# Moving a sum of squares from GpSimd to VectorE, and another order for the start of attention, in a two-block model on one core

## The reference, cut to what matters

```python
hx = modulate(rmsnorm(x, g), sh1, sc1)          # 512 x 1024
hc = modulate(rmsnorm(ctx, g), csh1, csc1)      # 256 x 1024
cq  = rmsnorm(hx @ w_dq, g_q)                   # 512 x 512
q   = (cq @ w_uq).reshape(16 heads, 64 + 32)    # the last 32 turned by position (rope)
kv  = hx @ w_dkv                                # 512 x 288, the same for hc
ckv = rmsnorm(kv[:, :256], g_kv)
k_pe = rope(kv[:, 256:])                        # one 32-wide part, shared by all heads
k   = concat(ckv @ w_uk, k_pe)                  # keys of context + x: 768
v   = ckv @ w_uv                                # 768 x 16 heads x 64
p   = softmax(q @ k.T / sqrt(96))               # per head, 512 x 768
x   = x + g1 * ((p @ v) @ w_o)
```

## Time and profile before

| | |
|---|---|
| median of 3 runs | 1750.52 us (1746.06 to 1751.31) |
| the profiled execution | 1746.06 us, its span 1744.3 us |
| mean granted TensorE clock | 0.993 |
| busy: PE, DVE, ACT, POOL | 98%, 59%, 32%, 58% |
| DMA | 217.19 MB, mean 125 GB/s |

### The profile page before, as it was taken

How to read it: one execution, slowest core, us unless ns; L and a number is a source line. 1 busy time by engine, 2 the same in 40 slices (tenths; PEclk the granted TensorE clock), 3 DMA queues, 4 the chain that set the end, 5 groups by cost and what they waited for, 6 DMA issues and landing times.

```text
span 1744.3 us, 24852 instructions
## 1 busy us (share of the span) xinstructions
PE 1708.5 (98%) x9190; PEld 1417.0 (81%) x9190; DVE 1027.0 (59%) x1514; ACT 560.4 (32%) x1019; POOL 1016.2 (58%) x675
## 2 busy tenths in 40 slices
PE   9999999999999999996999999999999999999998
PEld 7877888798888777786888898888888898787887
DVE  3456777677867743424487547655558259437183
ACT  4557777533233232112223124222212121113111
POOL 3447667556665665562666256666666634447663
PEclk9999999999999999998999999999999999999999
DMA  8223323133278853334223133334433362213332
GB/s 350 76 68 102 115 88 109 37 95 96 87 249 297 276 186 109 109 122 181 87 96 96 31 103 104 120 110 168 144 124 136 103 239 65 61 61 101 97 94 89
DMA packets 56183, 217.19 MB, mean 125 GB/s; under 512 B 6241, under 2 KB 8545, under 8 KB 53026
## 3 DMA queue, kind: packets, MB, share of 16 engines
q1 hardware_dynamic: 51058, 201.80, 34.5%
q10 hardware_dynamic: 5040, 14.22, 2.1%
HBM read 201.84 MB, written 14.16 MB: 124 GB/s over the span
## 4 chain that ended last, share of the span: by engine, by line
PE 91%; DVE 2%; POOL 2%; DMA 2%; ACT 1%; issue 1%; SPq 0%; POOLq 0%; DVEq 0%; ACTq 0%
PE PS L2010 27%; PE PS L2012 26%; PE PS L2011 26%; PE PS L2341 2%; PE PS L2357 2%; PE PS L770 2%; PE PS L1420 1%; POOL WL L1928 1%; DMA RAW<-in_whin 1%; PE PS L1404 1%; PE PS L557 1%; PE PS L1423 1%; PE PS L2164 0%; POOL WH L1925 0%; DMA X<-in_x 0%
## 5 line engine op out<-in xcount | busy, mean ns | idle before, releaser
L1928 POOL TENSOR_TENSOR WL<-RAW,WH 128x1024 fp32r<-128x1024 f32 (+3 forms) x233 | 599.3, 2572 | 19.4
L2010 PE MATMUL PS<-HH,WH 128*128 128x512 f32 (+1 forms) x1400 | 530.8, 379 | 19.4 <-POOL WL L1928 17.4
L2012 PE MATMUL PS<-HH,WL 128*128 128x512 f32 (+1 forms) x1400 | 525.2, 375 | 0.0
L2011 PE MATMUL PS<-HL,WH 128*128 128x512 f32 (+1 forms) x1400 | 525.0, 375 | 0.0
L1925 POOL TENSOR_SCALAR WH<-RAW 128x1024 fp32r<-128x1024 f32 (+3 forms) x233 | 258.4, 1109 | 331.6 <-PE PS L2012 297.0
L2010 PEld LDWEIGHTS PS<-HH,WH 128*128 128x128 f32 x1400 | 263.9, 189 | 76.7 <-POOL WL L1928 20.1
L2012 PEld LDWEIGHTS PS<-HH,WL 128*128 128x128 f32 x1400 | 263.9, 188 | 47.8
L2011 PEld LDWEIGHTS PS<-HL,WH 128*128 128x128 f32 x1400 | 264.1, 189 | 45.6
L1924 POOL TENSOR_TENSOR SC<-ONES 1x1 f32<-1x1 f32 x134 | 30.6, 229 | 286.3 <-PE PS L2012 261.5
L1953 POOL TENSOR_SCALAR PR<-PR,SC 128x768 f32<-128x768 f32 x47 | 109.5, 2337 | 69.8 <-DVE SC L3047 69.8
L2010 PE MATMUL PS<-HIDH,WH 128*128 128x512 f32 (+1 forms) x396 | 148.4, 375 | 0.0
(11 more groups left out here) (435 smaller groups left out, 2801.0 us busy)
## 6 DMA issues: line engine op xcount, KB each, us to landing
RAW<-in_wup SPq DMA_DIRECT2D x88, 512.0 KB, 3.6
MRF<-in_modw SPq DMA_DIRECT2D x52, 512.0 KB, 4.5
RAW<-in_wdn SPq DMA_DIRECT2D x32, 704.0 KB, 4.1
MR<-in_modw SPq DMA_DIRECT2D x28, 512.0 KB, 3.6
RAW<-in_whin SPq DMA_DIRECT2D x28, 512.0 KB, 3.6
MK<-in_modk SPq DMA_DIRECT2D x8, 1024.0 KB, 10.4
RAW<-in_whead SPq DMA_DIRECT2D x8, 640.0 KB, 4.6
RAW<-in_wo SPq DMA_DIRECT2D x8, 512.0 KB, 3.6
```

Source lines behind the costliest of these rows:

```text
L1928: pool.tensor_tensor(WL[s][:, 0:n], raw[:, 0:n], WH[s][:, 0:n].bitcast(F32), ALU.subtract).then_inc(tile_split, 1)
L2010: pe.matmul(out, wh, xh, start=first, stop=False)
L2011: pe.matmul(out, wh, xl, start=False, stop=False)
L2012: return pe.matmul(out, wl, xh, start=False, stop=last)
```

## The change

1. The sum of the four query squares is no longer made by POOL but by DVE, through bank 2 (a copy and three adds), and counted by `sq_add`. `query_input(2)` and `(3)` on ACT move behind the context's norm.
2. DVE does `turn_keys` ahead of `query(0)`, and `turned_keys_lo` ahead of `query_lo(0)`; ACT does the two copies of the turned keys ahead of `query_hi(0)` and `key_hi(0)`.
3. values(n) uses bank 4 + (n + 1) % 2; values(0) and values(1) both wait for `qready` 2, which `query_lo(0)` raises. The query of head 1 goes to bank 0 instead of 6 and waits for the third exponential of head 0.
4. PE's order up to the head loop changes, with three values ahead of score(0,0) instead of four, and `project_query(1)` behind score(0,3).
5. Head 0's probabilities are normalised by POOL alone (four tiles instead of two, ACT's two go), and the first `turn` waits for all four.

```diff
 query_bank:
-            return 6 if h == 1 else 4 + (h + 1) % 2
+            return 0 if h == 1 else 4 + (h + 1) % 2
 POOL:
-            for st, n in (("dq", 4), ("kv", 2)):
-                for j in range(n):
-                    split(st, j)
-            pool.wait_ge(S["cq_sq"], 4)
-            for j in range(1, 4):
-                pool.tensor_tensor(SSQA[:, 0:L], (CQS[0][:, :] if j == 1 else SSQA[:, 0:L]), CQS[j][:, :], ALU.add
-                                   ).then_inc(S["pchain"], 1)
-                if j < 3:
-                    pool.wait_ge(S["pchain"], 3 + j)
-            split("kv", 2)
-            for st, n in (("head0", 1), ("uv", 2)):
+            for st, n in (("dq", 4), ("kv", 3), ("head0", 1), ("uv", 2)):
                 for j in range(n):
                     split(st, j)
-                for qt in range(3 if h else 2):
+                for qt in range(3 if h else 4):
 PE:
-            pe.wait_ge(S["pchain"], 6)
+            pe.wait_ge(S["sq_add"], 4)
             stat("cq", blocks(L, SSQA))
 values(n):
-                if n == 1:
-                    pe.wait_ge(S["qready"], 2)
-                elif n >= 2:
-                    pe.wait_ge(S["v_ev"], n - 1)
-                out = bank(4 + n % 2)
+                pe.wait_ge(*((S["qready"], 2) if n < 2 else (S["v_ev"], n - 1)))
+                out = bank(4 + (n + 1) % 2)
 project_query(h, 0):
-                        pe.wait_ge(*((S["qready"], 4) if h else (S["nl"], NBASE["cq"] + 4)))
+                        pe.wait_ge(*((S["sexp"], 3) if h else (S["nl"], NBASE["cq"] + 4)))
 turn(h, 0):
-                    pe.wait_ge(S["pnorm"], 3 * h + 2)
-                    if h == 0:
-                        pe.wait_ge(S["kready"], 6)
+                    pe.wait_ge(S["pnorm"], 3 * h + 4)
 the order on PE:
             project_keys(0)
-            for n in range(4):
+            for n in range(3):
                 values(n)
             score(0, 0)
+            values(3)
+            score(0, 1)
             values(4)
-            score(0, 1)
+            score(0, 2)
+            score(0, 3)
             for k in range(4):
                 project_query(1, k)
-            score(0, 2)
-            values(5)
-            score(0, 3)
-            for n in range(6, 12):
+            for n in range(5, 12):
                 values(n)
 ACT:
-            for j in range(4):
-                query_input(j)
+            query_input(0)
+            query_input(1)
             root("ctx", D)
             diagonals("ctx", RTC)
             norm("ctx", HCH, LC)
+            query_input(2)
+            query_input(3)
             key_input(0, 0, L)
...
-            query_hi(0, S["kready"])
-            key_hi(0)
             act.wait_ge(S["krot"], 3)
             for hb in range(2):
                 act.copy(KPH[hb][hi, 0:L], PS[hi, 2, :]).then_inc(S["krot"], 1)
+            query_hi(0, S["kready"])
+            key_hi(0)
...
             query_hi(1, S["kready"])
-            normalise(0, qt=2)
-            normalise(0)
 DVE:
             norm("ctx", CTX, HCH, HCL, LC)
+            dve.wait_ge(S["cq_sq"], 4)
+            for j in range(4):
+                if j == 0:
+                    ins = dve.tensor_copy(bank(2), CQS[0][:, :])
+                else:
+                    dve.wait_ge(S["sq_add"], j)
+                    ins = dve.tensor_tensor(SSQA[:, 0:L] if j == 3 else bank(2), bank(2), CQS[j][:, :], ALU.add)
+                ins.then_inc(S["sq_add"], 1)
+
             dve.wait_ge(S["ckv_ev"], 6)
...
-            query(0)
             turn_keys()
+            query(0)
+            turned_keys_lo()
             query_lo(0)
-            turned_keys_lo()
             key_lo(0)
-            maximum(0, 0)
-            maximum(0, 1)
-            inverse_sum(0, 0)
+            for qt in range(4):
+                maximum(0, qt)
+                if qt:
+                    inverse_sum(0, qt - 1)
             query(1)
-            inverse_sum(0, 1)
-            maximum(0, 2)
-            maximum(0, 3)
-            inverse_sum(0, 2)
+            inverse_sum(0, 3)
             query_lo(1)
-            inverse_sum(0, 3)
```

More of the change, by code:

```diff
@@ L1470, in pe_second @@
                     pe.wait_ge(S["p2ev"], 23)
-                    pe.wait_ge(S["pchain"], 8)
+                    pe.wait_ge(S["pchain"], 5)
                 if k == 4:
@@ L1918, in split_at @@
                         ins.then_inc(*((tile_hi, 1) if c.start else (S["pchain"], 1)))
-                        pool.wait_ge(*((tile_hi, t + 1) if c.start else (S["pchain"], 7)))
+                        pool.wait_ge(*((tile_hi, t + 1) if c.start else (S["pchain"], 4)))
                         ins = pool.tensor_tensor(WL[s][:, c], raw[:, c], WH[s][:, c].bitcast(F32), ALU.subtract)
@@ L2259, in _ @@
             pe.wait_ge(S["ckv_ev"], 8)
-            pe.wait_ge(S["sq_add"], 1)
+            pe.wait_ge(S["sq_add"], 5)
             stat("ck", blocks(L, SSQK) + blocks(LC, SSQK[:, L:LK], SQT[:, L:LK]))
@@ L2568, in values @@
                     act.wait_ge(tile_done, FIRST_TILE["uv"] + n // 6 + 1)
-                act.copy(V[:, n % 6, 512 * (n // 6):512 * (n // 6) + 512], bank(4 + n % 2)
+                act.copy(V[:, n % 6, 512 * (n // 6):512 * (n // 6) + 512], bank(4 + (n + 1) % 2)
                          ).then_inc(S["v_ev"], 1)
@@ L2606, in out_hi, with normalise @@
                              PS[VH * half:VH * half + VH, 4 + h % 2, 0:256]).then_inc(S["ohi"], 1)
[L2608 to L2613, removed]
+            def normalise(h, i=0, per=0):
+                c = (4 * h + 3) % 8
+                act.wait_ge(S["rcp"], i * (4 * per) + (4 * h + 4))
+                act.activation(PR[h % 2][:, 3, :], PR[h % 2][:, 3, :], ACT.Identity, scale=RSUM[:, c:c + 1]
+                               ).then_inc(S["pt"], 2 if h == 15 else 1)
             def head(h, i=0, per=0):
@@ L2636, in _ @@
                 act.copy(KPH[hb][hi, 0:L], PS[hi, 2, :]).then_inc(S["krot"], 1)
+            query_hi(0, S["kready"])
+            key_hi(0)
             act.wait_ge(S["nl"], NBASE["ckc"] + 2)
-            for n in range(4):
+            for n in range(3):
                 values(n)
             exponential(0, 0)
+            values(3)
+            exponential(0, 1)
             values(4)
-            exponential(0, 1)
-            values(5)
             exponential(0, 2)
@@ L3031, in key_lo @@
                     r = slice(NOPE * hb, NOPE * hb + NOPE)
-                    dve.wait_ge(S["kready"], i * (2 * per) + (2 * p + 5 + hb if p else 2 + hb))
+                    dve.wait_ge(S["kready"], i * (2 * per) + (2 * p + 3 + hb if p else 2 + hb))
                     dve.tensor_tensor(KPL[hb][0:NOPE, :], keys_wide(p)[r, :], KPH[hb][0:NOPE, :].bitcast(F32),
@@ L3097, in _ @@
             dve.wait_ge(S["tab_in"], 48)
+            turn_keys()
             query(0)
-            turn_keys()
+            turned_keys_lo()
             query_lo(0)
-            turned_keys_lo()
             key_lo(0)
-            maximum(0, 0)
-            maximum(0, 1)
-            inverse_sum(0, 0)
+            for qt in range(4):
+                maximum(0, qt)
+                if qt:
+                    inverse_sum(0, qt - 1)
             query(1)
-            inverse_sum(0, 1)
-            maximum(0, 2)
-            maximum(0, 3)
-            inverse_sum(0, 2)
+            inverse_sum(0, 3)
             query_lo(1)
-            inverse_sum(0, 3)
             with repeat(dve, 3) as i:
```

## The result

| | before | after |
|---|---|---|
| median (4 runs each) | 1749.78 us (1746.06 to 1751.31) | 1764.91 us (1762.71 to 1766.62) |
| profiled execution, its span | 1746.06, 1744.3 us | 1763.2, 1761.4 us |
| mean granted TensorE clock | 0.993 | 0.987 |

The account below looks back on a forecast made before the run. PE's matmul starts were taken to bound the kernel. Waits of 2.0 us at the sum of squares and 7.0 at the start of attention made 9.0: 1759.5 us on the median 1750.5, range 1756 to 1763, 8 in 10 1755 to 1763.5.

Parts of the forecast that it names:

- What bounds the kernel: Whole kernel: PE holds 91% of the chain, so only later or earlier matmul starts count.
- Rival A: PE's long rest at 790.67 us swallows the delay, time stays 1750.5; chance 0.10 together with other losses by the way.
- Term one: Sum of squares, 50 to 76 us: DVE's later sum makes spread("cq") and all behind it 2.0 us late.
- the bound of 1.61: DVE's copy and three adds: 6.4 us in all if each takes 1.61, as an add beside POOL's split did.
- Term two: Start of attention: waits from values(0) on and POOL's chain make project_query(2) 7.0 us late.
- B: Wait ahead of values(0) is short, 4.06 us goes: 4.9 slower, 1755.4, within 0.3%; chance 0.05.
- D: Start of attention: PE runs through without waits, gaining 1.7 us net: 1748.8, within 0.3%; chance 0.03.
- The new rest of 4.06 us is a little shorter than those 4.5, so I count no fall: Rest ahead of values(0): PE's clock stays full, since it fell 4.5 us after the last work at 790.67; cost 0.
- part one: The sum of squares, 50 to 76 us, moved to DVE; forecast 2.0 us late.
- part two: The start of attention in its new order, up to project_query(2); forecast 7.0 us late.
- Rival C: Clock falls in the rest ahead of values(0), or POOL's split slows DVE's four steps: 1761 to 1763 us; chance 0.14.
- The rule of the Trainium skill: A few us of wait between matmul groups makes the next start at the low clock; sum 10.5 rather than 9.0.

Follow-up runs that it names:

- e0: The kernel before run once more, unchanged, for a second trace: 1748.38 us beside 1749.47, ratio 0.9997.
- e10: The kernel before with one idle ACT copy that lengthens PE's rest of 1.50 us ahead of values(8): 1751.89 us, ratio 1.0011.
- e4: The changed kernel with DVE's and ACT's order around the first query as before: 1759.78 us, ratio 1.0064.
- e7: The changed kernel with idle products (11, 18, 10, 9) ahead of stat("cq"), values(0), values(6) and project_query(2): 1758.55 us, ratio 1.0056.
- e5: The changed kernel with two of head 0's four normalisations back on ACT: 1763.26 us, ratio 1.0078.
- e2: The kernel before with only the sum of squares on DVE and query_input(2) and (3) behind the context norm: 1753.74 us, ratio 1.0024.
- e3: The kernel before with only the new order of attention, the sum of squares left on POOL: 1758.87 us, ratio 1.0057.
- e9: The changed kernel with idle products ahead of stat("cq"), values(0) and values(6), and two normalisations back on ACT: 1755.99 us, ratio 1.0039.
- e1: The changed kernel with longer idle products (14, 24, 12) ahead of stat("cq"), values(0) and values(6): 1764.47 us, ratio 1.0098.
- e8: The kernel before with ACT's normalisations behind values(7) and values(9), and 62 products of ones in the 15.19 us rest: 1745.58 us, ratio 0.9974.

## Why the prediction was wrong, point by point

- **What bounds the kernel:** right. PE is late by what it waits, and nothing absorbs it later. Rival A falls: PE came 15.55 late to the end of the long rest, and the rest was 15.08 against 15.19.
- **Term one, the waits:** right. Four DVE steps 2.88 (forecast 2.9), stat("cq") 2.55 late (2.6), spread("cq") 2.0 late with the clock full (2.0). The copy from SBUF took 0.69, near the adds with a PSUM operand, as chosen; the bound of 1.61 was not met, although POOL split from 71.71 to 75.19 beside the four.
- **Term two, the waits:** right. Ahead of values(0) 4.15 by the difference of starts, or 4.06 forecast; 1.12 (1.1) ahead of project_query(1); 2.27 (2.4) ahead of values(6); POOL's chain 16.48 (16.6). With the clock full 0.32 (0.5) at the first turn and 2.2 (2.3) at project_query(2). In the changed kernel these two shrank to nothing and 0.99: PE, slower behind values(6), used them up. Of the three low stretches the third therefore cost almost nothing, being hidden behind POOL's chain. Rivals B and D fall with this.
- **"The new rest of 4.06 us is a little shorter than those 4.5, so I count no fall":** this is the step that failed. It drew a limit out of one row: that the clock fell 4.5 us into the long rest before does not say that it needs 4.5. The same trace has a fall at 13.5 us behind no idle time over 0.39 (shown with e0). The changed kernel's clock fell 2.3 us into the rest of 4.00, and behind rests of 2.38 and 2.27 after PE was back at work. e10 shows a fall behind 2.28 in the kernel before, e4 one behind 1.84. Forecast for the clock was 0; measured are 1.4 (part one) and 2.2 (part two) in the profiled executions, 3.9 together by e7, 6 by the ratios. The prediction also asked about the rest ahead of values(0) alone, and not about the two of 2.4 us that it forecast itself.
- **Rival C** had this mechanism, at 0.14 and 1761 to 1763. Its size (1.5 to 3) fits the profiled execution's part two; it lacked the fall in part one. The rule of the Trainium skill that the prediction named (TensorE: Matmul & The Clock Gate, section HAM oscillation — how this bites in real kernels) was borne out by the rows at the rest of 4.00: the clock is at 0.50 at the first matmuls behind it. Behind the rests of 2.38 and 2.27 the first matmuls still ran at full clock. By it the sum was 10.5, nearer than 9.0, still short.
- **What is left:** the trace shows 12.6 in the stretch, the ratio says 12.8 to 18.5. e5 shows that part one's low stretch can cost 1.5 more than in the profiled execution of the changed kernel, which would bring 14.1, and e2's and e3's ratios sum to 0.0081, 14.2. That this spread is all of the difference is argued, not shown. The 1.1 before 805 us may be chance, as e0's shifts of that size are; the 1.4 behind it is the low clock of the old long rest, which e0 has as long without the change.

## What to carry to other kernels

A new rest of PE of about two us or more can have a second price behind it, matmuls at half clock (here 1.4 to 3 us a rest, less where another engine's chain hides it); price every one of them, and take no limit from a single row. Filler matmuls win it back only if they end before the producer does, and only in rests that set the end: here four well-fitted ones won 6 us of 15 by the ratios (3.9 in the traces), over-long ones nothing that the ratio shows. Where another engine's chain sets the end, its length and PE's clock hide each other, so two mends have to be tried together (0.8 us alone, 2.7 with the clock full).

## What the runs showed of the hardware

- The clock need not fall within the rest: in the changed kernel it fell 1.1 us after PE was back (at 76.5) and 0.8 after (at 124.3), in e4 1.9 after (at 76.0, behind a rest of 2.39) and 1.2 after (at 99.9). The first matmuls behind a rest at full clock are no proof that it was harmless.
- The length of the rest alone does not decide. Falls followed 1.84 (e4), 1.90 (e9), 2.05 (e10, at 551 us), 2.08 (e1), 2.27, 2.28 and 2.38; none followed 1.50 (before), 1.96 (e7) nor 2.11 (e8, behind 14 us of fillers). At the start the clock fell behind no idle time over 0.39 (before, 13.5 us).
- The length of the low stretch is not fixed: 3.4, 6.8 and 3.4 us in the profiled execution of the changed kernel, and in part one 3.4 there against 6.8 in e5, behind the same rest of 2.38.
- The copy of 512 columns from SBUF to PSUM takes DVE 0.69, and 0.73 from start to start, the same as an add with one PSUM operand. The add of two SBUF tiles (SSQK), 1.61 beside POOL's split before, took 0.68 in the changed kernel, where it starts at 75.21, when POOL's split has just ended.
